# The last expert's rows kept in SBUF and added by a selection matmul; gathers waiting for the last but one; two token tiles summed on VectorE

## What is computed

```
aff = sigmoid(t @ w_router)                      # t: 640 x 1024, 16 experts
idx = the two best experts of the best group     # per token
wsel = aff[idx] / sum(aff[idx])
y = sum over the two experts e of wsel_e * ((silu(t @ w_gate[e]) * (t @ w_up[e])) @ w_down[e])
x = x + g2 * y                                   # g2: one row for context, one for latent tokens
out = rms_norm(x, final_g)
```

## Time and profile before

| | |
|---|---|
| median of 3 runs | 722.83 us (722.69 to 723.99) |
| the profiled execution | 721.98 us |
| its span, first to last instruction | 720.1 us |
| mean granted TensorE clock | 0.992 |
| busy: TensorE, VectorE, ScalarE, GpSimd | 682.2, 232.1, 148.1, 149.6 us |
| HBM read and written | 163.13 and 22.31 MB |

### The profile page before, as it was taken

The page is one execution under the profiler, slowest core; times in us unless marked ns, Lnnn a source line. Parts: engine busy times, 40 slices in busy tenths (PEclk is TensorE's granted clock), DMA queues, the critical chain, the costliest instruction groups (busy, mean ns, idle before and its releaser), DMA issues.

```text
span 720.1 us, 12047 instructions
## 1 busy us (share of the span) xinstructions
PE 682.2 (95%) x5015; PEld 406.3 (56%) x5015; DVE 232.1 (32%) x512; ACT 148.1 (21%) x323; POOL 149.6 (21%) x182
## 2 busy tenths in 40 slices
PE   3899999999999999999899999999999999999894
PEld 2557646465457775544585455566546655654551
DVE  4310099900325763333486010110111011110137
ACT  6112101101256662121310010111101110111102
POOL 5137930900043531213111000000000000000050
PEclk9999999999999999999999999999999999999997
DMA  9994750609967333380655989799999999994183
GB/s 326 388 318 74 235 224 3 232 1 377 279 235 262 119 118 119 125 342 29 218 221 188 329 295 392 276 391 403 373 390 414 403 377 420 395 412 155 47 292 146
DMA packets 50824, 186.19 MB, mean 259 GB/s; under 512 B 7184, under 2 KB 9737, under 8 KB 46544
## 3 DMA queue, kind: packets, MB, share of 16 engines
q1 hardware_dynamic: 43568, 163.18, 60.6%
q0 software_dynamic: 7088, 22.17, 9.2%
q10 hardware_dynamic: 112, 0.04, 0.0%
HBM read 163.13 MB, written 22.31 MB: 258 GB/s over the span
## 4 chain that ended last, share of the span: by engine, by line
PE 87%; DMA 6%; DVE 4%; issue 1%; ACT 1%; SPq 0%; POOL 0%; DVEq 0%; ACTq 0%; POOLq 0%
PE bank L1814 12%; PE bank L1526 12%; PE bank L1821 10%; PE bank L1650 10%; PE bank L1837 6%; PE bank L1846 5%; PE bank L1589 5%; DMA slots<-in_w_ada 4%; PE bank L1471 3%; PE bank L1531 3%; PE bank L1829 3%; PE bank L1487 3%; PE bank L1684 2%; PE bank L1801 2%; PE bank L1854 2%
## 5 line engine op out<-in xcount | busy, mean ns | idle before, releaser
L1526 PE MATMUL bank<-ra,slots 128*128 128x512 f32 x192 | 83.3, 594 | 0.4 <-DVE ra L893 0.4
L1650 PE MATMUL bank<-slots,rc 128*128 128x512 f32 x160 | 69.9, 593 | 0.0
L1220 DVE TENSOR_TENSOR rc<-re,bank 128x256 f32<-128x256 f32 (+1 forms) x32 | 10.2, 359 | 160.6 <-PE bank L1821 88.3
L1526 PEld LDWEIGHTS bank<-ra,slots 128*128 128x128 f32 x192 | 36.1, 190 | 45.6 <-issue 44.6
L1414 POOL COPY gi<-ridx 128x1 uint32<-128x1 uint32 x16 | 3.0, 185 | 258.2 <-PE bank L1801 237.6
L1814 PE MATMUL bank<-rb,rc 128*128 128x512 f32 x128 | 56.2, 595 | 0.0
L570 ACT ACTIVATE rb<-bank 128x512 f32<-128x512 f32 (+1 forms) x64 | 30.3, 524 | 112.9 <-PE bank L1526 49.7
L908 DVE SCALAR_TENSOR_TENSOR re<-re,cwT 128x670 f32<-128x670 f32 x60 | 52.3, 948 | 0.0
L1650 PEld LDWEIGHTS bank<-slots,rc 128*128 128x128 f32 x160 | 29.9, 190 | 34.9 <-issue 34.9
L1305 POOL TENSOR_TENSOR mod<-mod,vecT 128x8 f32<-128x8 f32 (+1 forms) x8 | 19.6, 2455 | 122.8 <-ACT mod L570 122.8
L1821 PE MATMUL bank<-slots,rc 128*64 128x256 f32 x384 | 43.6, 381 | 0.0
(11 more groups left out here) (299 smaller groups left out, 987.2 us busy)
## 6 DMA issues: line engine op xcount, KB each, us to landing
slots<-in_w_ada SPq DMA_DIRECT2D x12, 2048.0 KB, 14.1
slots<-in_moe_w_gate SPq DMA_DIRECT2D x8, 2048.0 KB, 11.2
rb<-in_moe_w_gate SPq DMA_DIRECT2D x8, 2048.0 KB, 11.3
rb<-in_moe_w_up SPq DMA_DIRECT2D x8, 2048.0 KB, 12.9
rb<-in_moe_w_down SPq DMA_DIRECT2D x8, 2048.0 KB, 10.4
slots<-in_moe_w_up SPq DMA_DIRECT2D x8, 2048.0 KB, 12.5
slots<-in_moe_w_down SPq DMA_DIRECT2D x8, 2048.0 KB, 13.3
scratch_yd<-rb SPq DMA_DIRECT2D x1, 7680.0 KB, 21.3
```

Of the source, the lines that this page charges most:

```text
L1526: ins = mm(b[:, :], w[:, k, m * P:(m + 1) * P], hT[:, k, 0:NLAT], start=k == 0, stop=k == KD - 1)
L1650: ins = mm(b[:, :], mT[:, k, i * P:(i + 1) * P], wo[k // 4][:, k % 4, 512 * hf:512 * hf + 512], start=k == 4, stop=k == 3)
```

## The change

VISIT ends in 15, 5 instead of 5, 15, so that the last expert is one of 128 rows and the last but one has 64. The last expert's result is no longer stored: ScalarE copies both halves from PSUM to ylast in SBUF. Its rows of yd are among those set to zero early on. On VectorE, selection() builds during number 0 a weighted one-hot matrix of the tokens' rows in the last expert from rowhot, til and wts; TensorE transposes its five tiles during number 1, and ScalarE and VectorE copy them to picked. SyncE raises moe_stored when the last but one and those before it are stored.

At the end VectorE itself weights, adds, multiplies by g2 and adds to x the gathered rows of tiles 0 and 1 (FIRST = 2), after its last work for the last expert. TensorE runs 4 keep-warm calls; for each tile it multiplies picked with ylast, for tiles 2 to 4 on top of the diag matmuls. The sums use three pairs of banks in place of two.

```diff
--- before.py
+++ after.py
@@ -50,7 +50,7 @@
 CAP = [P] * 6 + [96] * 6 + [64] * 4
 EXTRA = 32
 WIDE = 2
-VISIT = [0, 1, 12, 2, 6, 7, 13, 3, 8, 9, 14, 4, 10, 11, 5, 15]
+VISIT = [0, 1, 12, 2, 6, 7, 13, 3, 8, 9, 14, 4, 10, 11, 15, 5]
 
 
 def most_overflow():
@@ -68,6 +68,7 @@
 MORE = NE + MAXOV
 BIG = MORE + 1
 WTILE = VISIT.index(WIDE)
+FIRST = 2
 RING = 6
 
 
@@ -310,6 +311,8 @@
     xt2 = ra[:, 4096:4352].rearrange("p (k n) -> p k n", k=KD)
     gs2, hid2, hidT2, yo2 = ra[:, 4352:4480], ra[:, 4480:4608], ra[:, 4608:4736], ra[:, 4736:4992]
     diag = rb[:, 14336:14336 + 2 * TT * P].rearrange("p (k c n) -> p k c n", k=2, c=TT)
+    picked = rb[:, 15616:15616 + NTOK]
+    ylast = ra[:, 3072:4096]
     pa_, pb_ = ra[:, 4096:4416], ra[:, 4416:4736]
     rw = re[:, 5120:5440]
 
@@ -319,7 +322,7 @@
         act_ready bm_ready smax_done pv_done spread_ready mixed_ready o_free expc_done mrow_out kcache_out vcache_out
         ssq2_ready ms2_ready sqrt2_ready hn_ready h2_ready h2_last tiles_hot rows_hot route_ready ridx_ready oi_ready
         xt_full xt_evac_a xt_evac_d gu_full silu_done hid_done hidT_full hidT_evac_a hidT_evac_d y_full y_evac_a y_evac_d bcend_in
-        diag_ready sum_ready x2_ready ssq3_ready ms3_ready sqrt3_ready rms3_ready out_ready out_done
+        sel_ready sel_full sel_evac_a sel_evac_d diag_ready sum_ready x2_ready ssq3_ready ms3_ready sqrt3_ready rms3_ready out_ready out_done
         more_in more_xt more_xt_evac more_silu more_hid more_hidT_evac more_y more_y_evac more_out
         zeros_ready zeros_out moe_stored over_stored gi_seen xg_seen gi_ready dve_chain pool_chain act_chain""".split()}
     w_slot = [sem(f"w_slot{i}") for i in range(3)]
@@ -400,7 +403,7 @@
 
     def pieces(n):
 
-        return {P: 1, 96: 6, 64: 2}[cap(n)]
+        return 0 if n == NE - 1 else {P: 1, 96: 6, 64: 2}[cap(n)]
 
     def stored(b, n):
 
@@ -449,6 +452,7 @@
                 sp.wait_ge(S["zeros_ready"], 1)
                 sp.dma_start(t["yd"][NE * P:BIG * P, :].rearrange("(q p) n -> p q n", p=P),
                              cuts[11].unsqueeze(1).to_broadcast([P, MAXOV + 1, D])).then_inc(S["zeros_out"], 16)
+                sp.dma_start(t["yd"][VISIT[-1] * P:(VISIT[-1] + 1) * P, :], cuts[11]).then_inc(S["zeros_out"], 16)
                 for c in (96, 64):
                     at_q = [q for q in range(NE) if CAP[q] == c]
                     rest = t["yd"][at_q[0] * P:(at_q[-1] + 1) * P, :].rearrange("(q p) n -> p q n", p=P)[c:P]
@@ -531,7 +535,8 @@
         for b in range(2):
             with sp.If(more > b):
                 load_more(b, NE - 2 + b, b)
-            store(b, NE - 2 + b)
+            if b == 0:
+                store(b, NE - 2)
 
         def over_pair(i):
             for b in range(2):
@@ -729,7 +734,7 @@
             b = filled(act, "aT", i)
             evac(mT[:, 0:4, i * P:(i + 1) * P], b[:, :].rearrange("p (m n) -> p m n", m=4))
 
-        act.wait_ge(S["zeros_out"], 16 * 3)
+        act.wait_ge(S["zeros_out"], 16 * 4)
         for j in range(STEPS):
             for s in (2 * j - 2, 2 * j - 1) if 1 <= j < PAIRS + 1 else ():
                 ge(act, "pv_done", j - 1)
@@ -807,6 +812,9 @@
             if wide:
                 sc.activation(gs2, bank[0][:, 0:P], ACT.Silu).then_inc(S["more_silu"], 1)
             xt_out(i + b, 1 - b)
+            if turn(i, b) == 1:
+                act.wait_ge(S["sel_full"], 1)
+                sc.activation(picked[:, 0:512], bank[4][:, :], ACT.Copy).then_inc(S["sel_evac_a"], 1)
             act.wait_ge(S["hidT_full"], i * 4 + (2 * b + 1))
             ge(act, "y_full", i * 4 + (2 * b - 2))
             w = 128 if c == 64 else 256
@@ -814,7 +822,12 @@
             act.wait_ge(S["y_full"], i * 4 + (2 * b + 1))
             ge(act, y_out[b], y_stored(i, b))
             w = 256 if c == 64 else 512
-            sc.activation(yo[:, b, 0:w], bank[4][:, 0:w], ACT.Copy).then_inc(S["y_evac_a"], 1)
+            if turn(i, b) == NE - 1:
+                sc.activation(ylast[:, 0:512], bank[4][:, :], ACT.Copy).then_inc(S["y_evac_a"], 1)
+                act.wait_ge(S["y_full"], 2 * NE)
+                sc.activation(ylast[:, 512:D], bank[5][:, :], ACT.Copy).then_inc(S["y_evac_d"], 1)
+            else:
+                sc.activation(yo[:, b, 0:w], bank[4][:, 0:w], ACT.Copy).then_inc(S["y_evac_a"], 1)
             if wide:
                 act.wait_ge(S["more_y"], 1)
                 sc.activation(yo2, bank[6][:, 0:256], ACT.Copy).then_inc(S["more_y_evac"], 1)
@@ -1210,6 +1223,15 @@
             v.tensor_copy(xt[:, b, 4:8, 0:c],
                           bank[1][:, :].rearrange("p (k n) -> p k n", k=4)[:, :, 0:c]).then_inc(S["xt_evac_d"], 1)
 
+        def selection():
+
+            mine = ov
+            link(v.tensor_scalar(mine, til, float(VISIT[-1]), None, ALU.is_equal))
+            link(v.tensor_tensor(mine, mine, wts[:, :, :], ALU.mult))
+            hots = rowhot.rearrange("p (k i) n -> p k i n", k=2)
+            link(v.tensor_tensor(hots, hots, mine.unsqueeze(3).to_broadcast([P, 2, TT, P]), ALU.mult))
+            v.tensor_tensor(hots[:, 0], hots[:, 0], hots[:, 1], ALU.add).then_inc(S["sel_ready"], 1)
+
         def tiles(i, b):
             c = cap(turn(i, b))
             dve.wait_ge(S["silu_done"], i * 2 + (b + 1))
@@ -1221,6 +1243,9 @@
             if turn(i, b) == WTILE:
                 dve.wait_ge(S["more_silu"], 1)
                 v.tensor_tensor(hid2, gs2, bank[1][:, 0:P], ALU.mult).then_inc(S["more_hid"], 1)
+            if turn(i, b) == 1:
+                dve.wait_ge(S["sel_full"], 1)
+                v.tensor_copy(picked[:, 512:NTOK], bank[5][:, 0:P]).then_inc(S["sel_evac_d"], 1)
             dve.wait_ge(S["hidT_full"], i * 4 + (2 * b + 2))
             ge(dve, "y_full", i * 4 + (2 * b - 2))
             a, w = {P: (256, 256), 96: (256, 128), 64: (128, 128)}[c]
@@ -1228,6 +1253,10 @@
             if turn(i, b) == WTILE:
                 v.tensor_copy(hidT2, bank[7][:, 256:384]).then_inc(S["more_hidT_evac"], 1)
             xt_out(i + b, 1 - b)
+            if turn(i, b) == 0:
+                selection()
+            if turn(i, b) == NE - 1:
+                return
             dve.wait_ge(S["y_full"], i * 4 + (2 * b + 2))
             ge(dve, y_out[b], y_stored(i, b))
             a, w = (256, 256) if c == 64 else (512, 256 if c == 96 else 512)
@@ -1250,13 +1279,19 @@
                                    ALU.mult, ALU.mult).then_inc(S["out_ready"], 1)
 
         dve.wait_ge(S["bcend_in"], 16 * 3)
+        for c in range(FIRST):
+            dve.wait_ge(fy_in[c], 32)
+            link(v.tensor_scalar(fy[:, c, 1, :], fy[:, c, 1, :], wts[:, 1, c:c + 1], None, ALU.mult))
+            link(v.scalar_tensor_tensor(fy[:, c, 0, :], fy[:, c, 0, :], wts[:, 0, c:c + 1], fy[:, c, 1, :], ALU.mult, ALU.add))
+            link(v.tensor_tensor(fy[:, c, 0, :], fy[:, c, 0, :], bc[:, 0, :], ALU.mult))
+            link(v.tensor_tensor(x[:, c, :], x[:, c, :], fy[:, c, 0, :], ALU.add))
         for c in range(TT):
             if c >= 1:
                 mean_square(c - 1)
             for hf in range(2):
                 dve.wait_ge(S["sum_ready"], 2 * c + hf + 1)
                 cols = slice(512 * hf, 512 * hf + 512)
-                link(v.tensor_tensor(fy[:, c, 0, cols], bank[(2, 6)[c % 2] + hf][:, :], bc[:, 0 if c < 4 else 1, cols], ALU.mult))
+                link(v.tensor_tensor(fy[:, c, 0, cols], bank[(2, 6, 0)[c % 3] + hf][:, :], bc[:, 0 if c < 4 else 1, cols], ALU.mult))
             if c >= 1:
                 inverse(c - 1)
             v.tensor_tensor(x[:, c, :], x[:, c, :], fy[:, c, 0, :], ALU.add).then_inc(S["x2_ready"], 1)
@@ -1911,6 +1946,13 @@
             if wide:
                 pe.wait_ge(S["more_silu"], 1)
             xT(i + b, 1 - b, 0)
+            if turn(i, b) == 1:
+                pe.wait_ge(S["sel_ready"], 1)
+                pe.wait_ge(S["y_evac_a"], 1)
+                pe.wait_ge(S["y_evac_d"], 1)
+                for q in range(4):
+                    nc.tensor.transpose(bank[4][:, q * P:(q + 1) * P], rowhot[:, q, :], ident)
+                nc.tensor.transpose(bank[5][:, 0:P], rowhot[:, 4, :], ident).then_inc(S["sel_full"], 1)
             if turn(i, b) == WTILE + 1:
                 pe.wait_ge(S["more_y_evac"], 1)
             ge(pe, "hidT_evac_a", i * 2 + b)
@@ -1927,6 +1969,9 @@
             wd = weights(i, b, 2)
             if turn(i, b) == 0:
                 emptied(pe, "table")
+            if turn(i, b) == 1:
+                pe.wait_ge(S["sel_evac_a"], 1)
+                pe.wait_ge(S["sel_evac_d"], 1)
             ht = hidT[:, b, :]
             ge(pe, "y_evac_a", i * 2 + b)
             ge(pe, "y_evac_d", i * 2 + b)
@@ -1953,16 +1998,20 @@
 
 
         pe.wait_ge(S["diag_ready"], 1)
-        keep_warm(36)
+        keep_warm(4)
         for c in range(TT):
-            pe.wait_ge(fy_in[c], 32)
+            if c >= FIRST:
+                pe.wait_ge(fy_in[c], 32)
             if c >= 2:
```

(13 more changed lines are left out.)

## The result

The changed kernel takes 716.07 us (median of 7 runs, 714.71 to 719.52), the kernel before 722.83 us in 7 runs; the ratio is 0.9914, 95% interval 0.9899 to 0.9929. It is faster, by 6.8 us where 10.5 were forecast, and lies 0.5 us above the upper end of the range. The profiled execution took 715.88 us with a span of 714.1, against the forecast span of 709.6.

A forecast was written before the change was run, and what follows sets the result against it. TensorE bounds nearly all the span, then a tail of store, gather and VectorE rounds. First add ends at 687.4 instead of 697.90, the remaining 22.2 us stay: 722.83 - 10.5 = 712.3 us; 8-in-10 range 710.8 to 715.6.

The forecast's parts named there:

- Gathers early, no one waits for them: Last expert: first gather issued at 661.3 to 666, all tiles landed by 684, before anyone asks for them.
- rival 3: End: gathers not early, presum waits for them, +6.7 us, 729.5; chance 0.03 fully, 0.02 in part.
- VectorE's presum: Before the main loop: VectorE sums tiles 0 and 1 from 675.5, 9.2 us, done at 684.7, setting the first product.
- rival 2: Presum on VectorE bounds more than thought (gap 2.4, slower links or held port): 1 to 3 us, 713.3 to 715.3; chance 0.10.
- The rest of the loop: Tiles 1 to 4: VectorE's 4.0 us rounds set the pace, TensorE needs 2.6 us for tiles 2 to 4; nothing gained or lost.
- TensorE's end: After the last down: 2.38 us gap, 0.9 us keep-warm, one matmul per half of tile 0; first sum ready at 684.2.
- The selection matrix: Experts 0 and 1: VectorE's 2.7 us hidden in a wait; transposes and copies delay TensorE 0.6 us, bounds 0.1 and 1.3.
- TensorE lost more than 1.3 us before its last down: Sign, ahead of the last down projection: a TensorE loss above 1.3 us would show the forecast wrong; 0.6 was counted.
- The swap: Last two experts exchanged: TensorE work sum stays, weights for down covered by 12 us at least; cost nothing.
- the zero store: SyncE's queue: 0.5 MB more ahead of a w_ada load, 2.7 us against slack of at least 5.2; cost nothing.
- Rival 1: Tail: TensorE falls to half clock after idling with fewer keep-warm calls, 2.3 to 2.5 us, 714.8; chance 0.12.

The follow-up runs named there:

- early tile 2: Changed kernel with tile 2's sums on TensorE started after VectorE's last copy of the expert loop, not after the first residual add: 712.65 us, ratio 0.9867.
- no_sel: Changed kernel without the five TensorE transposes of the selection matrix (copies stay and bring other data): 713.97 us, one execution.

## Why the forecast was too low, point by point

- **Gathers early, no one waits for them**: right; first gather 664.6, in the bounds of 661.3 to 666, and 4.4 us behind number 14's last matmul for 4.5. Its price when it fails (rival 3) was right too.
- **VectorE's presum**: right, 9.24 us for 9.2; its stepping over code 1.32 us for 1.5. It set the first product, as forecast, and rival 2 did not come.
- **The rest of the loop**: this step failed. The forecast has "TensorE needs 6 matmuls (2.6 us) for tiles 2 to 4". It took the duration of a record for that of a matmul; 6 matmuls are 12 records, 5.15 us, more than VectorE's 4.0. With the wait for the first add that cost 2.0 us of span. The timeline of before, 40 records for 20 matmuls, showed it. With 5.15 the same sum gives: tile 2 from 687.4, 15.5 us of sums, 8.3 us to the end, 711.2, 1.6 more.
- **TensorE's end**: two errors that stayed without effect. The gap behind the last down was 0.50 us, not 2.38, and the first half of tile 0 takes two records. In the kernel with early tile 2, where it could have mattered, VectorE's presum is later still.
- **The selection matrix**: 0.4 us on TensorE for 0.6, VectorE's part hidden. But the profiles with it lose 0.1 to 1.8 us more behind it, as the kernel before does when its code is moved. No row of before could show it; "TensorE lost more than 1.3 us before its last down" stood among what would make the forecast wrong.
- **The swap, the zero store**: nothing, as forecast; without the transposes the expert loop takes 303.2 us, against 303.4 to 303.5 in the kernel before. No wait for a load of the last two experts or the w_ada slice appears.
- **Rival 1, the clock**: it happens in some executions (tail 32.8 in the second profile and in no_sel, 31.2 and 31.1 in two others), worth 1.6 us where 2.3 to 2.5 were forecast, with a chance of 0.12. That price was worked out with the same halved matmul and with the low clock through tiles 2 to 4; in the second profile only tile 2's first four records are slow. The prediction held against it that the gap of 2.38 us left the clock at 1.00 in the kernel before. That was one profile: of six, the records behind that gap (2.0 to 2.7 us) are slow in three, here in the one shifted by 12 instructions, where 8.30 us is the time at full clock:

```profile
684.16 9.93 PE L1495 MATMUL bank<-cst 128*128 128x128 f32 x72 [2.28 <-issue]
```

The Trainium skill ("TensorE: Matmul & The Clock Gate", "What's actually happening") has idle time bring the half clock. The trace agrees in these profiles and not in the others, in which the clock stayed at 1.00 over a gap of the same length.

Together for the profiled run: the first expert 1.6 us late by the clock (the profile of before had it early, at 376.15), 1.1 us more in the expert loop than the 0.6 counted, 1.9 us in the tail make the 4.5 between 709.6 and 714.1. On medians the tail gives 9.2 or, at the low clock, 7.6 us and the loop takes back about 1.7.

## What to carry to other kernels

Count records before you multiply: divide the count of a row by the number of instructions in the source, and check that the product gives the duration of the whole group. When work moves from a wait into the open, price both engines of the new loop again, because the one that was slack before (TensorE at 3.4 of 4.0 us) is the bound after a small addition, and look at each wait that paces it. Keep-warm work is free only while something else is awaited.

## What was not expected of the hardware

With TensorE's code shifted by 12 instructions, a loop that the shift doesn't touch took 1.9 us more, with a shift by 20 nothing and by 32 0.3, in one profile each. The low clock after an idle gap of 2.0 to 2.7 us on TensorE came in five profiles of ten: three of six of the kernel before, two of four of the changed one; after the gaps of up to 1.7 us in the tails of the other variants it did not come. The keep-warm matmuls ahead of the first expert ran at a granted clock between 0.50 and 1.00, other from one execution to the next, and the start moves by some 2 us (375.9 to 378.0). GpSimd's issue of an indirect gather is stretched from 0.94 to 1.71 us by a multiply-add on VectorE, and not by an add, though both read two operands in SBUF.
